# A two-block transformer kernel on one core: first gemm by passes, splits, context rows and stores in another order

## The chip, the cores and the metric

The kernel runs on one core of a Trainium2 chip. The time is that of the whole program on the device, in microseconds (us), as the median of several runs; less is better. A core has TensorE (PE in the profile; its weight loads are PEld), VectorE (DVE), ScalarE (ACT), GpSimd (POOL) and SyncE (SP), each with its own instructions in program order, tied together by semaphores. DMA queues bring data from memory to the on-chip SBUF. PE writes its products into eight PSUM banks.

## The reference

The inputs are float32. The first block takes x (256 rows of 1024) and computes, with an input norm, one projection `w_in` to six parts, chunkwise retention of 8 heads on q, k, v, a gated linear recurrence (RG-LRU) behind a causal convolution, and a product with `w_out` plus residual and a norm:

```python
xn = rms_norm(h, norm_in_g)
proj = einsum('btd,de->bte', xn, w_in)
...
h = h + einsum('bte,ed->btd', concatenate([y_ret, y_lru]), w_out)
return rms_norm(h, norm_out_g)
```

The second block has two layers over these 256 latent rows and 256 context rows. Each layer makes six modulation vectors (shift, scale and gain, twice) from the conditions, `silu(c) @ w_mod[l] + b_mod[l]`; then

```python
h = modulate(rms_norm_2(x, g_pre_mix[l]), sh1, sc1)
...(mLSTM, grouped attention and neighbourhood attention on h @ w_in[l])
o = merge_branches(y_ml, y_ga, y_na, zg, w_branch[l], w_out[l])
x = x + ga1 * rms_norm_2(o, g_post_mix[l])
f = conv_ffn(modulate(rms_norm_2(x, g_pre_ffn[l]), sh2, sc2), ...)
x = x + ga2 * rms_norm_2(f, g_post_ffn[l])
```

and the same for the context rows in layer 0. Layer 1 needs the latent rows alone behind its keys and values. The product of `ga` and the post-norm's weight is the "post-norm gain": a vector of 1024 for each of the latent and context rows (in layer 1, of the latent rows only).

## The kernel before

**Precision and pieces.** Every large product is done as three: both operands are split into a high part (fp32r) and the rest, and PE adds hi*hi, hi*rest and rest*hi. The weights come as a stream of 356 pieces of 512 KB (128 x 1024 float32, two blocks of 128 input rows by 512 columns) into a ring of four slots. SP issues a piece when the piece four before has been split to its low part (L728). ACT makes w_hi (`split_hi`, L1323; it waits for the piece to have landed and for PE to have used the piece four before), DVE makes w_lo (`split_lo`, L1959; it waits for w_hi). `split_hi(n)` makes all pieces below n that are not made yet, `ahead(key)` does so up to what PE needs soon. PE's `gemm` (matmul at L787) goes piece by piece, and for each pair of blocks does the three products one behind the other, so it needs w_hi, w_lo and both input parts before a piece. `gemm_by_groups` (L939), which serves the first w_in_2 chunks of a layer, goes in passes over a piece instead (all hi*hi, then the others), with norm transposes `norm_T` (L890, L892) between the groups.

**Order.** The order of every engine is written out by hand; nothing is planned at run time. The stages are: norm and w_in of the first block (to about 158 us), with retention and RG-LRU interleaved; w_out of the first block (to about 210 us); layer 0; layer 1 (from about 1100 us). Modulation vectors are made on DVE (L2015) from weight rows `mod_w` and `c_rows`, wherever DVE has room.

**Start.** PE warms up with WARM transposes of zeros (L824) and transposes the normed rows xn1 (L831), made on DVE in four halves (L1979). ACT evicts them to xT_hi (L1345) and DVE makes xT_lo (L1987), with a piece's split between any two. Then ACT does the recurrence's constants (L1347 to L1351), the split up to RING + 1 = 5 pieces, and silu of the conditions c_rows (L1354), for which DVE's first modulation products wait.

**First block's end.** Retention head h goes through DVE's statistics, ACT's root (`ret_sqrt`, L1410), DVE's norm and gate, PE's transposes (L871), ACT's `ret_mix` (L1416, mix_hi) and DVE's `ret_lo` (L2122, mix_lo). Pieces 48 to 63 are w_out. The context rows come by a DMA that ACT issues (L1490) after ret_sqrt(7); their squares and roots (L1497, L1499) stand on ACT after ret_mix(7), and `norm_right` on DVE (L2324, L2331; the right half row, and the reciprocal for the left half that ACT's `norm_left` L1505 makes) after the last retention head.

**Banks.** `take` (L597) hands out PSUM banks in rotation, six of them (0 to 5) for gemms, and waits until the bank has been drained. In the merge, `zg` chunks and branch products `br` take two banks each in turn; DVE drains the latter in `branch` (L2955, L2957).

**Post-norm gains.** DVE computes `gcol` (`post_gains`, L2312), 128 x 8 values per row kind. SP stores them transposed to memory (L701), as 1024 single elements of four bytes, behind the piece that `store_at` names, and reads them back as whole rows for all partitions (L714) behind the piece that `load_at` names, when they are wanted.

## Time and profile before

| | before |
|---|---|
| median of 3 runs | 1673.6 us |
| lowest and highest | 1673.26 and 1674.83 us |
| profiled execution, its own time | 1677.26 us |
| its span in the trace | 1675.6 us |
| busy PE / DVE / ACT | 1660.5 / 1240.1 / 847.2 us |

The profile is one execution. Its span runs from the first to the last instruction; the own time has 1.66 us around it. Busy time counts an engine's instructions; matmuls overlap, so a row with 0.28 us for a matmul of 256 columns can have the next one 0.12 us later. A row of the timeline has the start and the length in us, the engine, the line, the operation, what it writes and reads, its size and how many are run together; in brackets the idle time before it and what ended it. "Clock" is the granted clock of PE as a share of 2.4 GHz.

### The profile page before, as it was taken

To read this page: it belongs to the slowest core of one execution; us is meant where nothing else is said; L and a number is where in the kernel's file an instruction comes from. 1 tells how busy PE (TensorE), PEld (TensorE's weight loads), DVE (VectorE), ACT (ScalarE), POOL (GpSimd) and SP (SyncE) were. 2 spreads that over 40 slices of the span, in tenths; PEclk is the share of its full clock that TensorE was granted. 3 is DMA by queue.
4 is the path that set the end of the run, shared out by engine and by line. 5 is a ranking of instruction groups with operands and counts; after the bars stand their busy time and mean duration, and the time that the engine had idled before them with its cause. 6 is when DMAs were issued, how large, how long until landed. Compare 5 with 4: busy or idle time off the path is not lost.

```text
span 1675.6 us, 25213 instructions
## 1 busy us (share of the span) xinstructions
PE 1660.5 (99%) x9808; PEld 1426.9 (85%) x9808; DVE 1240.1 (74%) x2160; ACT 847.2 (51%) x1382; POOL 0.2 (0%) x4
## 2 busy tenths in 40 slices
PE   9999999999999999999999999999999999999998
PEld 9898888778887778889888888889788999989997
DVE  7999967966778897857878775347756776677874
ACT  6666555554334443256444442347553465575653
POOL 0000000000000000000000000000000000000000
PEclk9999999999999999999999999999999999999999
DMA  8657643132235346524555555324323554547563
GB/s 335 242 202 262 240 140 113 64 126 76 67 106 187 114 146 204 207 80 138 132 186 186 188 186 202 101 68 159 89 82 64 139 158 153 187 151 168 185 202 125
DMA packets 80230, 258.03 MB, mean 154 GB/s; under 512 B 14448, under 2 KB 18800, under 8 KB 79472
## 3 DMA queue, kind: packets, MB, share of 16 engines
q1 hardware_dynamic: 74352, 248.02, 45.8%
q10 hardware_dynamic: 5760, 8.39, 1.5%
q8 instruction: 79, 1.29, 0.3%
q14 instruction: 39, 0.32, 0.1%
HBM read 255.31 MB, written 1.07 MB: 153 GB/s over the span
## 4 chain that ended last, share of the span: by engine, by line
PE 89%; DVE 5%; ACT 3%; issue 1%; DMA 1%; ACTq 0%; DVEq 0%
PE bank L787 74%; PE bank L939 3%; PE bank L1117 2%; PE bank L1133 2%; PE bank L1105 2%; PE bank L1213 2%; DVE w_lo L1959 2%; ACT w_hi L1323 1%; DMA w_raw<-in_weights 1%; PE bank L1199 1%; DVE mod_w L2015 1%; DVE xc L2058 1%; PE bank L824 0%; PE bank L892 0%; PE bank L890 0%
## 5 line engine op out<-in xcount | busy, mean ns | idle before, releaser
L1959 DVE TENSOR_TENSOR w_lo<-w_raw,w_hi 128x1024 fp32r<-128x1024 f32 (+1 forms) x356 | 427.8, 1211 | 247.9 <-ACT w_hi L1323 246.5
L1323 ACT ACTIVATE w_hi<-w_raw 128x1024 fp32r<-128x1024 f32 (+1 forms) x356 | 370.1, 1048 | 335.7 <-PE bank L787 277.4
L787 PE MATMUL bank<-hT_hi,w_hi 128*128 128x512 f32 (+1 forms) x1280 | 447.5, 350 | 2.8 <-ACT w_hi L1323 2.3
L787 PE MATMUL bank<-hT_hi,w_lo 128*128 128x512 f32 (+1 forms) x1280 | 438.2, 342 | 0.0
L787 PE MATMUL bank<-hT_lo,w_hi 128*128 128x512 f32 (+1 forms) x1280 | 437.9, 342 | 0.0
L787 PEld LDWEIGHTS bank<-hT_hi,w_hi 128*128 128x128 f32 x1280 | 243.3, 190 | 31.1 <-ACT w_hi L1323 2.4
L787 PEld LDWEIGHTS bank<-hT_hi,w_lo 128*128 128x128 f32 x1280 | 243.2, 190 | 28.2
L787 PEld LDWEIGHTS bank<-hT_lo,w_hi 128*128 128x128 f32 x1280 | 243.5, 190 | 27.2 <-issue 1.0
L2015 DVE SCALAR_TENSOR_TENSOR mod_w<-mod_w,c_rows 128x1024 f32<-128x1024 f32 x102 | 124.3, 1219 | 8.5 <-DMA mod_w<-in_mod_weights 8.3
L787 PE MATMUL bank<-w_hi,hT_hi 128*128 128x512 f32 x272 | 114.3, 420 | 0.0
L787 PE MATMUL bank<-w_lo,hT_hi 128*128 128x512 f32 x272 | 106.7, 392 | 0.0
L787 PE MATMUL bank<-w_hi,hT_lo 128*128 128x512 f32 x272 | 106.5, 391 | 0.0
L2984 DVE SCALAR_TENSOR_TENSOR conv<-bank,vec,conv 128x510 f32<-128x510 f32 (+1 forms) x176 | 103.1, 612 | 3.5
L787 PE MATMUL bank<-w_hi,fT_lo 128*128 128x512 f32 x264 | 102.7, 389 | 0.0
L787 PE MATMUL bank<-w_hi,fT_hi 128*128 128x512 f32 x264 | 102.7, 389 | 0.0
L787 PE MATMUL bank<-w_lo,fT_hi 128*128 128x512 f32 x264 | 102.7, 389 | 0.0
L787 PE MATMUL bank<-xT_hi,w_hi 128*128 128x256 f32 x256 | 73.6, 287 | 1.8 <-DVE w_lo L1959 1.1
L787 PE MATMUL bank<-xT_hi,w_lo 128*128 128x256 f32 x256 | 72.4, 283 | 0.0
L787 PE MATMUL bank<-xT_lo,w_hi 128*128 128x256 f32 x256 | 72.4, 283 | 0.0
L1930 ACT ACTIVATE conv<-bank,vec 128x512 f32<-128x512 f32 (+1 forms) x88 | 56.1, 669 | 27.9 <-PE bank L787 26.6
L787 PE MATMUL bank<-yT_hi,w_hi 128*128 128x512 f32 (+1 forms) x192 | 66.6, 347 | 0.0
L2623 DVE TENSOR_REDUCE att<-bank 128x1 f32<-128x512 f32 (+1 forms) x96 | 54.6, 596 | 15.9 <-PE bank L1105 14.7
(399 smaller groups left out, 2707.7 us busy)
## 6 DMA issues: line engine op xcount, KB each, us to landing
w_raw<-in_weights SPq DMA_DIRECT2D x356, 512.0 KB, 4.2
mod_w<-in_mod_weights SPq DMA_DIRECT2D x102, 512.0 KB, 4.0
nbias<-in_window_bias ACTq DMA_DIRECT2D x32, 128.0 KB, 3.1
resid_c<-in_ctx ACTq DMA_DIRECT2D x2, 1024.0 KB, 5.5
gain_mix<-gain_rows SPq DMA_DIRECT2D x3, 512.0 KB, 5.7
gain_ffn<-gain_rows SPq DMA_DIRECT2D x3, 512.0 KB, 4.6
c_rows<-in_conditions SPq DMA_DIRECT2D x1, 1024.0 KB, 5.8
gatew<-in_gate_weights SPq DMA_DIRECT2D x1, 1024.0 KB, 11.4
```

The lines of the kernel that those rows point to most:

```text
L787: mm = pe.matmul(held[key][:, oc], st, mv_, start=(opens and k == 0 and t == 0 and i == 0), stop=(closes and k == tiles - 1 and t == 2), s ...
L939: mm = pe.matmul(held[key][:, o], st, mv_, start=opens, stop=(k == KD - 1 and t == 2), skip_group_check=True)
L1105: mm = pe.matmul(ps[j][:, score_at(g, t)], q_of(kind, q_lo, g + j, cols), k_of(kind, k_lo, g + j, n), start=(i == 0 and g == h), stop=(i = ...
L1117: mm = pe.transpose(ps[:, j * P:(j + 1) * P], prob[:, prob_of(h, t), j * P:(j + 1) * P], ident)
L1133: mm = pe.matmul(ps[i * HD:(i + 1) * HD, e // 2 * P:(e // 2 + 1) * P], v_[:, j, g * HD:(g + 1) * HD], turned_of(kind, l, e + i, t)[:, j * ...
L1213: mm = pe.matmul(ps[:, j * (P + 1):(j + 1) * (P + 1)], ml_w[:, d, s, t * P:(t + 1) * P], mv[:, s, h, :], start=(s == keys[0]), stop=(s == ...
L1323: a.activation(w_hi[:, p % RING, :, used], w_raw[:, p % RING, :].rearrange("p (k n) -> p k n", k=KP)[:, :, used], ACT.Copy).then_inc(hi_re ...
L1930: a.activation(conv[:, q, conv_cols(c)], psum(key)[:, j * nq:(j + 1) * nq], ACT.Identity, scale=V(f"ffn_w{l}", 2 * FB + blk), bias=V(f"ffn ...
L1959: v.tensor_tensor(w_lo[:, p % RING, :, used], w_raw[:, p % RING, :].rearrange("p (k n) -> p k n", k=KP)[:, :, used], w_hi[:, p % RING, :, ...
L2015: mm = v.scalar_tensor_tensor(product, w, 1.0, c_rows[:, s, :], ALU.mult, ALU.mult, accum_out=modT[:, l, j, s:s + 1])
L2623: v.tensor_reduce(att[:, h % 4, 0:1], ps[:, score_at(h, t)], AX.X, ALU.max, negate=True)\
L2984: v.scalar_tensor_tensor(dst, src, V(f"ffn_w{l}", tap * 2 * FB + blk), dst, ALU.mult, ALU.add)\
```

## The change

It has these parts, in the order of the diff.

- Start: WARM is 22 instead of 24. The left half of the second tile of xn1 is made on ACT, and the transposes wait for it. The first gemm, ("in", 0), is done by `gemm_first`: a piece in three passes (hi*hi, hi*rest, rest*hi), each with its own wait. On DVE, xT_lo stands ahead of w_lo for each pair.
- Pieces and conditions: ACT splits up to RING + 2 = 6 pieces ahead of silu of c_rows, and DVE splits the same ahead of the modulation products.
- Stores: in layer 1 the mix store goes behind piece ("w_in_2", 1, 4) instead of ("w_in_2", 1, 9), and the ffn store behind ("w_in_2", 1, 5) instead of ("w_up", 1, 4). The ffn gains use column 1 of gcol and are computed with the mix gains.
- Passes of `gemm_by_groups`: (0, "mix") takes hi*hi, hi*rest, rest*hi, where it took hi*hi, rest*hi, hi*rest. The others stay.
- Banks: the rotation is set to 4 ahead of merge(2).
- Context: the load is issued after ret_sqrt(6) instead of ret_sqrt(7); squares and roots stand ahead of split_hi(56), ret_mix(6) and ret_mix(7); the squares go to xn1 instead of sg. `norm_right` stands ahead of ret_lo(7).

```diff
@@ -120,7 +120,7 @@
 FIRST_MERGE = stream().index(("w_in_2", 0, 9, 0))
-WARM = 24
+WARM = 22
@@ -353,6 +353,11 @@
+    def gain_column(l, which):
...
+        return 1 if l and which == "ffn" else 0
...
@@ -698,13 +705,13 @@
                 for c in range(n):
-                    sp.dma_start(gain_rows[gain_index(l, which), c, :, :].rearrange("k p -> p k"), gcol[:, :, c], allow_slow_non_contiguous=True)\
+                    sp.dma_start(gain_rows[gain_index(l, which), c, :, :].rearrange("k p -> p k"), gcol[:, :, gain_column(l, which) + c], allow_slow_non_contiguous=True)\
...
-                sp.wait_ge(gain_stored, 16 * gain_loads(l, which))
+                sp.wait_ge(gain_stored, 16 * gain_loads(l, "ffn" if l else which))
@@ -715,9 +722,9 @@
             for l in range(LAYERS):
-                store_at[piece("w_in_2", l, 9)] = l, "mix"
+                store_at[piece("w_in_2", l, 4 if l else 9)] = l, "mix"
                 load_at[piece("w_out_2", 0, 0) + 4 if l == 0 else piece("w_in_2", l, 13) + 4] = l, "mix"
-                store_at[piece("w_up", l, 4)] = l, "ffn"
+                store_at[piece("w_in_2", l, 5) if l else piece("w_up", l, 4)] = l, "ffn"
@@ -825,6 +832,8 @@
                 pe.wait_ge(*xn_ready.at(("b1", g // 2)))
+                if g == 0:
+                    pe.wait_ge(*xn_left.at(0))
@@ -832,6 +841,34 @@
+            def gemm_first(banks):
...
+                at, n = pieces[0], KD // KP
+                for p in range(n):
+                    s = (at + p) % RING
+                    pieces[0] = at + p + 1
+                    pe.wait_ge(hi_ready, at + p + 1)
+                    pe.wait_ge(*xT_hi_ready.at(p))
+                    for t, (w, x) in enumerate(((w_hi, xT_hi), (w_hi, xT_lo), (w_lo, xT_hi))):
+                        if t == 1:
+                            pe.wait_ge(*xT_ready.at(p))
+                        if t == 2:
+                            pe.wait_ge(lo_ready, at + p + 1)
+                        for key, subs in banks:
+                            ps = psum(key) if p or t else take(pe, key)
+                            for i, (oc, wc, xcols) in enumerate(subs):
+                                for kk in range(KP):
+                                    k = p * KP + kk
+                                    mm = pe.matmul(ps[:, oc], w[:, s, kk, wc], x[:, k, xcols], start=(k == 0 and t == 0 and i == 0),
+                                                   stop=(k == KD - 1 and t == 2), skip_group_check=True)
+                            if t == 2 and key == banks[-1][0]:
+                                mm.then_inc(piece_used, 1)
+                                plan[("filled", key)] = ("piece", 0, at + n, at + n)
+                            elif t == 2 and p == n - 1:
+                                mm.then_inc(*filled(key))
+                                b, count = plan[("filled", key)][1:3]
+                                plan[("filled", key)] = ("bank", b, count, at + n)
@@ -903,7 +940,7 @@
                 whole, rest_x, rest_w = (w_hi, hT_hi), (w_hi, hT_lo), (w_lo, hT_hi)
-                passes = (whole, rest_x, rest_w) if l and which == "ffn" else (whole, rest_w, rest_x)
+                passes = (whole, rest_w, rest_x) if (l, which) in ((0, "ffn"), (1, "mix")) else (whole, rest_x, rest_w)
@@ -1020,7 +1057,7 @@
             late = Beside(retention_late(), RET_EVERY // 2, 2 * RET_SKIP)
-            gemm_T(("in", 0), xs, xT_hi, xT_lo, inputs=xT_ready.at)
+            gemm_first(blocks_T(("in", 0), 4, None, xs))
@@ -1265,6 +1302,7 @@
                 na.finish()
+                turn["rot"] = 4
@@ -1335,6 +1373,8 @@
             a.activation(rs[:, 0:2], ss[:, 0:2], ACT.Sqrt, scale=1.0 / D, bias=eps[:]).then_inc(*A.tell(root_ready, "b1"))
+            act.wait_ge(*xn_inv.at(0))
+            a.activation(xn1[:, 1, 0:COLS], resid[1][:, 1, 0:COLS], ACT.Copy, scale=rs[:, 3:4]).then_inc(*A.tell(xn_left, 0))
@@ -1349,7 +1389,7 @@
             a.activation(lam[:, 2, :], lam[:, 1, :], ACT.Ln, bias=1.0).then_inc(*A.tell(lam_ready, 0))
-            split_hi(RING + 1)
+            split_hi(RING + 2)
@@ -1482,22 +1522,22 @@
             ret_sqrt(6, False)
+            act.wait_ge(*drained_at(("rs", HEADS - 1)))
+            act.dma_start(resid[0][:], ctx_in).then_inc(ctx_loaded, 16)
...
             ret_sqrt(7, False)
-            act.wait_ge(*drained_at(("rs", HEADS - 1)))
-            act.dma_start(resid[0][:], ctx_in).then_inc(ctx_loaded, 16)
+            act.wait_ge(ctx_loaded, 16)
+            for t in range(NT):
+                a.activation(xn1[:, t, :], resid[0][:, t, :], ACT.Square, accum_out=ss[:, 56 + t:57 + t]).then_inc(*A.next())
+                act.wait_ge(*A.last())
+                a.activation(rs[:, 56 + t:57 + t], ss[:, 56 + t:57 + t], ACT.Sqrt, scale=1.0 / D, bias=eps[:])\
+                    .then_inc(*A.tell(root_ready, (0, "mix", t)))
...
             ret_mix(7)
-            split_hi(LAST_OUT)
-            act.wait_ge(ctx_loaded, 16)
-            for t in range(NT):
-                a.activation(sg[:, t, :], resid[0][:, t, :], ACT.Square, accum_out=ss[:, 56 + t:57 + t]).then_inc(*A.next())
-                act.wait_ge(*A.last())
-                a.activation(rs[:, 56 + t:57 + t], ss[:, 56 + t:57 + t], ACT.Sqrt, scale=1.0 / D, bias=eps[:])\
-                    .then_inc(*A.tell(root_ready, (0, "mix", t)))
@@ -1528,6 +1568,7 @@
                 norm_left(0, "mix", t)
+            split_hi(LAST_OUT)
@@ -1971,15 +2012,13 @@
             dve.wait_ge(*root_ready.at("b1"))
-            v.reciprocal(rs[:, 2:4], rs[:, 0:2]).then_inc(*W.next())
+            v.reciprocal(rs[:, 2:4], rs[:, 0:2]).then_inc(*W.tell(xn_inv, 0))
             dve.wait_ge(*W.last())
-            for half in range(2):
+            for half, t in ((0, 0), (1, 0), (1, 1)):
                 cols = slice(half * COLS, (half + 1) * COLS)
-                for t in range(NT):
-                    v.tensor_scalar(xn1[:, t, cols], resid[1][:, t, cols], rs[:, 2 + t:3 + t], None, ALU.mult)\
-                        .then_inc(*(W.tell(xn_ready, ("b1", half)) if t == NT - 1 else W.next()))
+                v.tensor_scalar(xn1[:, t, cols], resid[1][:, t, cols], rs[:, 2 + t:3 + t], None, ALU.mult)\
+                    .then_inc(*(W.tell(xn_ready, ("b1", half)) if t == half else W.next()))
             for g in range(KD // 2):
-                split_lo(g + 1)
@@ -1988,6 +2027,7 @@
                 W.mark(xT_ready, g)
+                split_lo(g + 1)
@@ -2156,6 +2196,7 @@
             split_lo(RING + 1)
+            split_lo(RING + 2)
@@ -2294,9 +2335,7 @@
             mod_ops(1)
-            ret_lo(7)
-            mod_ops(1)
-            mod_bias(0, 0, 16, 2, EARLY_MODS)
@@ -2314,8 +2353,8 @@
                 g_post = V(f"g_post_{which}{l}", 0, KD)
-                n = 2 if l == 0 else 1
-                v.tensor_tensor(gcol[:, :, 0:n], modT[:, l, 8 * (o + 2):8 * (o + 3), 0:n],
+                n, c0 = 2 if l == 0 else 1, gain_column(l, which)
+                v.tensor_tensor(gcol[:, :, c0:c0 + n], modT[:, l, 8 * (o + 2):8 * (o + 3), 0:n],
@@ -2368,11 +2407,15 @@
+            for t in range(NT):
+                norm_right(0, "mix", t)
+            ret_lo(7)
+            mod_ops(1)
+            mod_bias(0, 0, 16, 2, EARLY_MODS)
...
             norm_gains(0, "mix")
-            for t in range(NT):
-                norm_right(0, "mix", t)
             split_lo(LAST_OUT)
+            dve.wait_ge(*W.last())
@@ -2449,7 +2492,10 @@
                     norm_gains(*nxt)
-                    post_gains(*nxt)
+                    if nxt != (1, "ffn"):
+                        post_gains(*nxt)
+                    if nxt == (1, "mix"):
+                        post_gains(1, "ffn")
```

## Rows read from the trace of the kernel before

**Rows 1.** Page, part 1: engine, busy us (share), instructions.

```profile
PE 1660.5 (99%) x9808; PEld 1426.9 (85%) x9808; DVE 1240.1 (74%) x2160; ACT 847.2 (51%) x1382; POOL 0.2 (0%) x4
```

**Rows 2.** Waits of PE: line, what ended it, us, times, longest.

```profile
PE bank L787 <- ACT w_hi L1323: 2.3, 1, 2.3
...
PE bank L787 <- DVE w_lo L1959: 1.1, 3, 0.6
...
PE bank L939 <- DVE w_lo L1959: 0.9, 2, 0.5
```

**Rows 3.** Timeline, PE near 1525: start, length, instruction, idle before it.

```profile
1524.96 0.28 PE L787 MATMUL bank<-hT_hi,w_lo 128*128 128x256 f32 x1
1527.49 0.35 PE L787 MATMUL bank<-hT_hi,w_hi 128*128 128x256 f32 x1 [2.25 <-ACT w_hi L1323]
```

**Rows 4.** The same, ACT.

```profile
1523.95 1.06 ACT L1323 ACTIVATE w_hi<-w_raw 128x1024 fp32r<-128x1024 f32 x1 [7.71 <-DMA w_raw<-in_weights]
```

**Rows 5.** The same, SyncE's queue near 1510.

```profile
1510.15 0.43 SPq L701 DMA_DIRECT2D gain_rows<-gcol  x1
```

**Rows 6.** Stretches: each engine's busy us, granted clock, DMA share, GB/s.

```profile
1290.00:1304.00 14.00, 14.00 (x78) 12.12 (x77) 7.69 (x20) 3.06 (x4) 0.00 (x0) 1.00 0.83 65
...
1510.60:1523.90 13.30, 13.30 (x114) 13.30 (x113) 6.65 (x12) 4.56 (x7) 0.00 (x0) 1.00 1.02 102
...
1528.65:1532.06 3.41, 3.41 (x19) 3.41 (x18) 3.37 (x8) 3.29 (x7) 0.00 (x0) 0.50 0.77 245
```

**Rows 7.** Page, part 6: DMA issues, median us to landing.

```profile
w_raw<-in_weights SPq DMA_DIRECT2D x356, 512.0 KB, 4.2
```

**Rows 8.** Timeline, ACT in attention of layer 1.

```profile
1169.82 1.06 ACT L1323 ACTIVATE w_hi<-w_raw 128x1024 fp32r<-128x1024 f32 x1 [3.98 <-PE bank L787]
...
1188.59 1.06 ACT L1323 ACTIVATE w_hi<-w_raw 128x1024 fp32r<-128x1024 f32 x1
```

**Rows 9.** The same, DVE.

```profile
1188.74 0.69 DVE L2663 TENSOR_TENSOR gkT_lo<-bank,gkT_hi 128x512 fp32r<-128x512 f32 x1 [2.52 <-ACT gkT_hi L1792]
```

**Rows 10.** The same, PE.

```profile
1189.53 0.51 PE L1105 MATMUL bank<-gkT_hi,gqT_hi 64*128 64x512 f32 x2
```

**Rows 11.** Timeline, PE at layer 1's third merge.

```profile
1416.22 0.36 PE L787 MATMUL bank<-hT_hi,w_hi 128*128 128x256 f32 x1 [0.52 <-DVE ptmp L2955]
```

**Rows 12.** Timeline, PE in the first gemms.

```profile
11.68 0.35 PE L787 MATMUL bank<-xT_hi,w_hi 128*128 128x256 f32 x1 [0.78 <-DVE xT_lo L1987]
...
59.20 0.36 PE L787 MATMUL bank<-xT_hi,w_hi 128*128 128x256 f32 x1 [0.59 <-DVE w_lo L1959]
```

**Rows 13.** The same, DVE.

```profile
22.84 1.23 DVE L2015 SCALAR_TENSOR_TENSOR probT<-mod_w,c_rows 128x1024 f32<-128x1024 f32 x1 [2.00 <-ACT c_rows L1354]
```

**Rows 14.** Timeline, ACT, root of retention head 6.

```profile
175.83 0.20 ACT L1410 ACTIVATE bnst<-bnst 128x2 f32<-128x2 f32 x1 [2.85 <-DVE bnst L2094]
```

**Rows 15.** DMA issues between 180 and 190 us.

```profile
resid_c<-in_ctx ACTq DMA_DIRECT2D x1, 1024.0 KB, 6.3
```

**Rows 16.** Stretch with the context's squares and roots on ACT, as in 6.

```profile
193.45:196.31 2.86, 2.86 (x15) 2.33 (x13) 2.56 (x9) 2.77 (x7) 0.00 (x0) 1.00 0.96 339
```

**Rows 17.** Timeline, DVE, 185 to 197 us.

```profile
185.69 1.22 DVE L1959 TENSOR_TENSOR w_lo<-w_raw,w_hi 128x1024 fp32r<-128x1024 f32 x1
...
190.78 2.36 DVE L1959 TENSOR_TENSOR w_lo<-w_raw,w_hi 128x1024 fp32r<-128x1024 f32 x2
...
195.48 0.15 DVE L2324 RECIPROCAL ss<-rs 128x1 f32<-128x1 f32 x1
...
196.91 2.36 DVE L1959 TENSOR_TENSOR w_lo<-w_raw,w_hi 128x1024 fp32r<-128x1024 f32 x2
```

**Rows 18.** Timeline, PE, out product and first w_in_2 groups.

```profile
192.11 0.47 PE L787 MATMUL bank<-w_hi,mix_hi 128*128 128x512 f32 x1 [0.30 <-issue]
...
220.31 0.76 PE L939 MATMUL bank<-w_lo,hT_hi 128*128 128x272 f32 x4 [0.55 <-DVE w_lo L1959]
...
221.83 0.84 PE L890 MATMUL bank<-tab,sg 128*128 128x128 f32 x6 [0.26 <-ACT sg L1505]
```

More of the change, by code:

```diff
@@ L572, in build @@
     xn_ready = Counter("xn_ready")
+    xn_inv = Counter("xn_inv")
+    xn_left = Counter("xn_left")
     diag_ready = Counter("diag_ready")
@@ L588, in build @@
                qk_root, qk_ss, resid_ready, ret_hi, ret_root, ret_var, ret_y, root_ready, rows_ready, xT_hi_ready,
-               xT_ready, xn_ready, diag_ready, inv_ready, left_ready, right_ready, yT_hi_ready, yT_ready, gcol_ready, stat_ready, zo_ready, eps_ready)
+               xT_ready, xn_ready, xn_inv, xn_left, diag_ready, inv_ready, left_ready, right_ready, yT_hi_ready, yT_ready, gcol_ready, stat_ready, zo_ready, eps_ready)
     by_name = {c.name: c.sem for c in signals}
```

## The prediction

> **What bounds the kernel now.** I read the page first. TensorE (PE) is busy for 1660.5 us of a span of 1675.6, VectorE (DVE) for 1240 and ScalarE (ACT) for 847 [rows 1]. No edit takes a matmul away, save two of warm-up. So a change can only win time in which PE stands still or runs slowly, and that is 15 us at most, half of it before the first weight arrives. The second view is what PE waited for [rows 2]: one wait of 2.3 us for w_hi, three of 1.1 in sum and two of 0.9 in sum for w_lo, and little else. The third is PE's own order of time at each of these places, the fourth the engines that fed it there, and the last the stretches with DMA share and clock.
>
> The largest loss is late. A matmul starts at 1524.96 and the next at 1527.49, where 0.12 is the normal distance: 2.4 us lost [rows 3]. ACT had stood idle for 7.71 us until 1523.95, waiting for a weight piece from memory [rows 4]. SyncE had issued a post-norm store, gain_rows<-gcol, at 1510.15, right behind that piece [rows 5]. While it is under way the DMA engines are busy with a share of 1.02 and yet move only 102 GB/s [rows 6]: the store writes 1024 single elements of four bytes. The piece issued just ahead of it needed about 14 us (1509.8 to 1523.95), where a piece needs 4.2 in the median [rows 7]. Behind this gap PE runs for 3.41 us at a granted clock of 0.50, the lower level of 1.2 GHz [rows 6], half of which is lost: 1.7.
>
> **Part 1, the post-norm stores.** Layer 1's ffn store goes from the fifth w_up piece (1510) to a w_in_2 piece near 1177, its mix store from near 1290 to near 1161, one w_in_2 piece apart. At the old place nothing else is near: the 2.4 and the 1.7 go, **-4.1 us**. Next there is late nothing; pieces would land in their 4.2 us with ACT free. The old mix store cost no time: from 1290 to 1304 the share is 0.83 at 65 GB/s, and PE is busy for all 14.00 us [rows 6]. In the new place both stores come where a piece serves PE for a long time, since attention is interleaved: ACT's splits stand at 1169.82 (idle 3.98 us before, for PE) and 1188.59 [rows 8]. With the 14 us of a hit piece, the one issued at some 1161 lands near 1176 instead of 1166, the next one or two near 1178 and 1191. ACT works in program order, so the query copies gqT_hi behind the first of these splits and the key copies behind the third would be later, and there is no reserve: DVE makes the last low part of the keys from 1188.74 to 1189.43 [rows 9], and PE's first scores start at 1189.53 [rows 10]. Below: 0. Above: a stall and a clock loss as at 1527 for each store, 2 x 4.1. I take 0, by the store at 1290, because PE needs the piece issued at 1161 only at about 1188. The small extra product for column 1 of gcol is a DVE instruction of some 0.15 us (as the reciprocal in [rows 17]) beside slack.
>
> The Trainium skill, "DMA: Bandwidth & Descriptors", section "Why small descriptors are slow (HBM only)", speaks against this part: it names a fixed overhead of about three bus cycles for each packet and 32 bytes of metadata for each descriptor. By an estimate from that page, 1024 such elements over 16 engines are well under a microsecond of work, the 14 us would not be the store's, and the sum would be +0.8 instead of -3.3. The share of 1.02 at 102 GB/s and at 0.83 with 65 GB/s behind both stores [rows 6] says otherwise.
>
> **Part 2, bank order.** With turn["rot"]=4 before merge(2), layer 1's first zg chunk of the third merge no longer takes the two banks that the branch product has just filled. PE waited 0.52 us for the DVE drain there, and the first matmul after it took 0.08 longer [rows 11]: **-0.6**. In layer 0 the order turns as well, but the banks it now meets were drained 1 to 2 us before; 0, and at most the same 0.6 the other way.
>
> **Part 3, the start.** By passes, the first gemm needs only xT_hi and w_hi, so the 0.78 us of waiting for xT_lo [rows 12] goes, and the left half row of the second tile, made on ACT, takes an operation of about 0.5 off DVE (a norm_right is one with a reciprocal of 0.15 before it, and two take 1.28, [rows 17]) ahead of the transposes: 1.2 us earlier. But from 22.84 on DVE works without a break up to about 64 us, and the three waits for w_lo at L787 of [rows 2] lie in that stretch, the last and longest at 59.20 [rows 12]: the end of DVE's chain sets PE, not its start. What the chain starts with is silu of the conditions, for which DVE is idle 2.00 us [rows 13]. The sixth piece's split on ACT, 1.06 (as in [rows 4]), now stands ahead of it: chain +1.1. Its w_lo on DVE, 1.2, moves into that idle time: chain -1.2. Together 0. Swapping xT_lo ahead of w_lo also ends the first w_lo 0.9 to 1.6 later, and with them pieces five to eight are issued later, all inside the same hidden stretch if they land before 20. Bounds: -1.2 (advance kept) and +0.6 (the sixth piece lands late and holds silu). I take **0**: a 1.2 won at 11 and given back by 38 and 59 us.
>
> **Part 4, context load, squares, rows.** The load of the context is issued behind the sixth ret_sqrt, which ends at 176.03 [rows 14], and takes 6.3 us [rows 15]: landed 182.3. ACT now waits for it before w_hi of piece 55 and does squares and roots first, 2.86 us [rows 16]: to 185.1, then the split to 186.2. Queued behind the waiting instruction are that split, ret_mix(6) and the pieces after. DVE began w_lo of that piece at 185.69 [rows 17]: +0.5. Then the two norm_right, 195.48 to 196.91 less 0.15 idle = 1.28 [rows 17], stand ahead of ret_lo(7), and so ahead of the pair of w_lo at 190.78, the first of which PE awaited when it began piece 56 at 192.11 (0.30 idle) [rows 18]. PE starts there 0.5 + 1.3 = 1.7 later, near 193.8. About 0.3 comes back, as the rows that PE takes 6 us later are now ready early. What follows to the second tile of layer 0 (out product, residual, rows, transposes, 221.83 [rows 18]) is a chain from PE itself and moves along. **+1.4 us**. Bounds: -1.1 (waits of 0.30, 0.55 and 0.26 in [rows 18] vanish, nothing is added) and +2.
>
> **Part 5, pass order of the first w_in_2 groups.** (0, mix) now takes the third product (w_lo) last, so the 0.55 at 220.31 [rows 18] goes; but the next thing PE needs is the rows at 221.83, which are as late as before: 0 by itself, bounds -0.5 and +0.3 (hT_lo late in its place). Removed waits and the emptied warm-up cost nothing.
>
> **Sum**, for the profiled execution of 1677.26 us (span 1675.6 and 1.66 around it): -4.1 - 0.6 + 0 + 1.4 + 0 = -3.3, so 1673.9 to 1674.0. That execution stands 3.66 us above the median of the runs, 1673.6. If the difference is the profiler's, the median becomes 1670.3.
>
> **Rivals.**
> - *The late stall is not in ordinary runs.* 3.66 above the median is close to 4.1. For it: a landing time is what varies most. Against: the store's 1024 elements are issued in every run. Without any of it, -0.6 + 1.4 = +0.8: 1674.4; with the gap but no clock loss, -1.6: 1672.0. Chance 0.22.
> - *The middle and start win too.* The waits of [rows 18] vanish (-1.1) and the start keeps its 1.2: -4.1 - 0.6 - 1.1 - 1.2 = -7.0: 1666.6. For it: the waits stand there, and an earlier row or split is what ends each. Against: DVE has no gap to give it. Chance 0.20.
> - *Slower: the moved stores block ACT in layer 1's attention.* The piece ahead of each store takes 14 us, ACT stands in program order before gqT_hi and gkT_hi, and PE, with 0.1 of reserve at 1189.53, stalls and falls to 1.2 GHz. One such stall as at 1527 gives the 4.1 back: +0.8, 1674.4, no change. Two give +4.9, 1678.5. It decides from a piece at 1161 that lands after 1172. For it: two stores within 16 us. Against: [rows 6], the store at 1290 with PE busy throughout. Chance 0.13 for slower than the bound below.
> - *The start does not do what it says*, 1.2 up to 38 us and nothing after: that is in the forecast.
>
> **How the numbers follow.** 0.2% is 3.35 us, about what runs of this kernel can tell from no change: 1670.25 to 1676.95. Forecast 0.45 at 1670.3, which stands on the border, so half of it (0.22) is faster and half the same. Faster: 0.22 + 0.20 = 0.43. Same: 0.22 + 0.20 of the first rival = 0.43. Slower: the third and a rest of the first, 0.14. The range goes from the second rival's 1666.6 to 1674.6, just over the first rival's end, and leaves out 0.14 above and some 0.05 below. The forecast's own range is 1668.8 to 1672.2.
>
> **What would show it.** In the changed kernel's trace: no wait for w_hi over 1 us after 1500 and a granted clock of 1.00 there (part 1); no wait for ptmp in layer 1's merge (part 2); first weight matmul at 10.5 but the wait for w_lo near 38 and 59 longer (part 3); piece 56 begun at 193.8 with over 1.5 us of waiting for w_lo (part 4); no w_lo wait in (0, mix), one for the rows (part 5). The prediction is wrong if that piece begins before 192.5, if the time up to 100 us is over 0.8 shorter, or if PE waits over 1 us between 1165 and 1225.

## The result, and the profile after

Over 22 runs of each, the changed kernel takes 1678.26 us in the median (1674.94 to 1680.44) and the kernel before 1674.05 (1672.45 to 1677.55): ratio 1.0023, 95% interval 1.0017 to 1.0029. It is slower by 4.2 us, where 3.3 us faster was forecast. Yet the profiled executions stand the other way: 1676.76 us (span 1675.0) after, 1677.26 (span 1675.6) before. So the two traces can't be compared by their ends; they are compared stretch by stretch.

The page of the changed kernel, parts 1 and 6:

```profile
span 1675.0 us, 25206 instructions
PE 1658.2 (99%) x9804; PEld 1425.3 (85%) x9804; DVE 1239.4 (74%) x2159; ACT 848.8 (51%) x1383; POOL 0.2 (0%) x4
...
c_rows<-in_conditions SPq DMA_DIRECT2D x1, 1024.0 KB, 7.1
```

Its waits of PE, to be read against [rows 2] (L794 was L787, L976 was L939, L927 was L890):

```profile
PE bank L794 <- issue: 3.7, 2, 3.1
PE bank L794 <- DVE w_lo L2000: 2.7, 4, 1.1
...
PE bank L927 <- ACT sg L1545: 0.7, 1, 0.7
PE bank L976 <- DVE w_lo L2000: 0.4, 1, 0.4
```

The wait of 2.3 us for w_hi is gone, and in its place stands one of 3.1 us, and 2.7 instead of 1.1 for w_lo. PE's timeline has the places:

```profile
10.48 0.36 PE L863 MATMUL bank<-xT_hi,w_hi 128*128 128x256 f32 x1
...
29.09 0.36 PE L794 MATMUL bank<-xT_hi,w_hi 128*128 128x256 f32 x1 [1.09 <-DVE w_lo L2000]
...
60.65 0.35 PE L794 MATMUL bank<-xT_hi,w_hi 128*128 128x256 f32 x1 [0.58 <-DVE w_lo L2000]
...
196.31 0.47 PE L794 MATMUL bank<-w_hi,mix_hi 128*128 128x512 f32 x1 [3.14 <-issue]
...
225.75 0.52 PE L927 MATMUL bank<-tab,sg 128*128 128x128 f32 x3 [0.75 <-ACT sg L1545]
...
1193.43 0.50 PE L1142 MATMUL bank<-gkT_hi,gqT_hi 64*128 64x512 f32 x2
```

The first matmul is 1.2 us earlier than in [rows 12]; at 60.65 PE is 1.45 late, at 196.31 (against 192.11 in [rows 18]) 4.2, at 225.75 (221.83) 3.9, and at 1193.43 (1189.53, [rows 10]) still 3.9. The loss is made in two places, 11 to 60 us and 176 to 196 us. In layer 1 the third merge has no wait for ptmp as in [rows 11], which is worth 0.8 (PE's lateness falls from 3.9 to 3.1), and near 1525 there is no stall and no slow clock as in [rows 3] and [rows 6] (-4.0): 3.9 - 0.8 - 4.0 = -0.9. ACT's last read of a bank starts at 1668.89 instead of 1669.74, 0.85 earlier, of which the spans keep 0.6.

**Start.** The issues of the conditions and of the sixth piece by SyncE, before and after:

```profile
11.15 0.43 SPq L734 DMA_DIRECT2D c_rows<-in_conditions  x1
12.71 0.33 SPq L728 DMA_DIRECT2D w_raw<-in_weights  x1
```

```profile
12.73 0.43 SPq L741 DMA_DIRECT2D c_rows<-in_conditions  x1
14.28 0.33 SPq L735 DMA_DIRECT2D w_raw<-in_weights  x1
```

The sixth piece landed at 18.3 (5.6 us after its issue) before and at 21.1 (6.8 us) after. ACT, then DVE, of the changed kernel:

```profile
21.11 1.06 ACT L1361 ACTIVATE w_hi<-w_raw 128x1024 fp32r<-128x1024 f32 x1 [1.70 <-DMA w_raw<-in_weights]
22.19 1.28 ACT L1394 ACT_TABLE_LOAD   x1
23.48 1.92 ACT L1394 ACTIVATE c_rows<-c_rows 128x2048 f32<-128x2048 f32 x1
```

```profile
22.20 1.22 DVE L2000 TENSOR_TENSOR w_lo<-w_raw,w_hi 128x1024 fp32r<-128x1024 f32 x1 [1.54 <-ACT w_hi L1361]
25.43 1.23 DVE L2055 SCALAR_TENSOR_TENSOR probT<-mod_w,c_rows 128x1024 f32<-128x1024 f32 x1 [2.00 <-ACT c_rows L1394]
```

ACT waits 1.70 us for the sixth piece, with silu behind it in program order. DVE's chain starts at 25.43 instead of 22.84 [rows 13]: 2.6 late, less the one w_lo now done before it, 1.14: 1.45, the delay at 60.65. It is more than executions differ by: this wait ends at 60.15 to 60.89 in the five traces with the whole new start (after, e1, e13 to e15) and at 58.48 to 59.62 in the eleven with the old one.

**Middle.** ACT and DVE:

```profile
184.88 1.06 ACT L1533 ACTIVATE xn<-resid_c 128x1024 f32<-128x1024 f32 x1 [1.43 <-DMA resid_c<-in_ctx]
...
187.63 1.04 ACT L1361 ACTIVATE w_hi<-w_raw 128x1024 fp32r<-128x1024 f32 x1
```

```profile
188.71 1.22 DVE L2000 TENSOR_TENSOR w_lo<-w_raw,w_hi 128x1024 fp32r<-128x1024 f32 x1 [1.59 <-ACT w_hi L1361]
...
195.00 2.35 DVE L2000 TENSOR_TENSOR w_lo<-w_raw,w_hi 128x1024 fp32r<-128x1024 f32 x2
```

The context landed at 184.86, 7.7 us after its issue at 177.19, not 6.3. All that the forecast queued behind it follows: w_hi of piece 55 at 187.63, DVE idle 1.59, the first w_lo of the pair done at 196.1, PE at 196.31. DVE's 1.59 and the 1.2 of the two half rows (193.81 to 195.00) make the 2.75 us that PE loses here on top of the start's 1.45.

### The profile page after: what moved, and what is told of

Its sections match the earlier page's. It is cut to its first block, busy times and chain, and to the rows that moved or that the text cites. A ratio compares the mean times of both kernels' runs of the same rounds, so it can differ in the third digit from the quotient of the medians.

```text
span 1675.0 us, 25206 instructions
## 1 busy us (share of the span) xinstructions
PE 1658.2 (99%) x9804; PEld 1425.3 (85%) x9804; DVE 1239.4 (74%) x2159; ACT 848.8 (51%) x1383; POOL 0.2 (0%) x4
## 4 chain that ended last, share of the span: by engine, by line
PE 90%; DVE 5%; ACT 2%; issue 1%; DMA 0%; ACTq 0%; DVEq 0%
PE bank L794 75%; PE bank L976 3%; PE bank L1154 2%; PE bank L1170 2%; PE bank L1142 2%; PE bank L1250 2%; DVE w_lo L2000 1%; PE bank L1236 1%; ACT w_hi L1361 1%; DVE mod_w L2055 1%; DVE xc L2098 1%; PE bank L831 0%; PE bank L929 0%; PE bank L927 0%; DMA w_raw<-in_weights 0%
## 5 line engine op out<-in xcount | busy, mean ns | idle before, releaser
L794 PE MATMUL bank<-hT_hi,w_hi 128*128 128x512 f32 (+1 forms) x1280 | 446.6, 349 | 0.0
L794 PE MATMUL bank<-hT_hi,w_lo 128*128 128x512 f32 (+1 forms) x1280 | 437.6, 342 | 0.0
L794 PE MATMUL bank<-hT_lo,w_hi 128*128 128x512 f32 (+1 forms) x1280 | 437.3, 342 | 0.0
L794 PEld LDWEIGHTS bank<-hT_hi,w_hi 128*128 128x128 f32 x1280 | 242.6, 190 | 28.1 <-issue 1.7
L794 PEld LDWEIGHTS bank<-hT_hi,w_lo 128*128 128x128 f32 x1280 | 242.5, 189 | 28.2
L794 PEld LDWEIGHTS bank<-hT_lo,w_hi 128*128 128x128 f32 x1280 | 242.8, 190 | 27.0 <-issue 1.0
L794 PE MATMUL bank<-w_hi,hT_hi 128*128 128x512 f32 x272 | 114.3, 420 | 0.0
L794 PE MATMUL bank<-w_lo,hT_hi 128*128 128x512 f32 x272 | 106.7, 392 | 0.0
L794 PE MATMUL bank<-w_hi,hT_lo 128*128 128x512 f32 x272 | 106.5, 391 | 0.0
L794 PE MATMUL bank<-w_hi,fT_hi 128*128 128x512 f32 x264 | 102.7, 389 | 0.0
L794 PE MATMUL bank<-w_hi,fT_lo 128*128 128x512 f32 x264 | 102.7, 389 | 0.0
L794 PE MATMUL bank<-w_lo,fT_hi 128*128 128x512 f32 x264 | 102.7, 389 | 0.0
L794 PE MATMUL bank<-xT_hi,w_hi 128*128 128x256 f32 x224 | 64.6, 288 | 3.3 <-DVE w_lo L2000 2.7
L794 PE MATMUL bank<-yT_hi,w_hi 128*128 128x512 f32 (+1 forms) x192 | 66.6, 347 | 0.0
L794 PE MATMUL bank<-yT_hi,w_lo 128*128 128x512 f32 (+1 forms) x192 | 64.7, 337 | 0.0
L794 PE MATMUL bank<-yT_lo,w_hi 128*128 128x512 f32 (+1 forms) x192 | 64.6, 336 | 0.0
```

Of the source, the lines that this page charges most:

```text
L794: mm = pe.matmul(held[key][:, oc], st, mv_, start=(opens and k == 0 and t == 0 and i == 0), stop=(closes and k == tiles - 1 and t == 2), s ...
```

## Experiments

Ratios are of medians to before, measured beside it on the same chip in five rounds, with the 95% interval in brackets. There were four such sessions, in which the kernel before had medians of 1674.45 (e1 to e4), 1673.96 (e5 to e8), 1674.13 (e9 to e12) and 1674.03 us (e13 to e16); a difference in us is to the one of its own session. Each experiment starts from the kernel before unless it says otherwise.

**e1_start: the start alone.** Edit, all hunks of the start, in short:

```diff
-WARM = 24
+WARM = 22
...
-            gemm_T(("in", 0), xs, xT_hi, xT_lo, inputs=xT_ready.at)
+            gemm_first(blocks_T(("in", 0), 4, None, xs))
...
-            split_hi(RING + 1)
+            split_hi(RING + 2)
...
-                split_lo(g + 1)
...
                 W.mark(xT_ready, g)
+                split_lo(g + 1)
```

> The start of the changed kernel alone (passes, left half row on ACT, low part of the inputs ahead of the low part of the weights, sixth piece ahead of the conditions); all else as before. Theory A (from the two traces: the sixth piece lands at 21.1 instead of 18.3 us, so silu of the conditions ends 2.5 us later and the vector engine's chain behind it 1.4 later): +1.4 us against before, and the third wait for w_lo ends near 60.6 instead of 59.2. Rival B (the start is neutral, as forecast; the loss in the trace of the changed kernel is an accident of that execution): 0 us, third wait ends near 59.2.

1678.7 us, ratio 1.0023 (1.0013 to 1.0034): +4.2 us, three times what theory A expected. PE's timeline:

```profile
60.81 0.36 PE L789 MATMUL bank<-xT_hi,w_hi 128*128 128x256 f32 x1 [0.58 <-DVE w_lo L1993]
...
201.61 0.41 PE L922 MATMUL bank<-tab,sg 128*128 128x128 f32 x2 [2.17 <-ACT sg L1539]
```

The 60.81 is theory A's. The 2.17 is new: in the old order the context's squares stand on ACT behind splits of weight pieces, and those pieces landed late beside the context, which took 8.6 us itself (ACT waited 6.04, 1.23 and 0.19 us for pieces between 186 and 196 us). That wait of PE is in the kernel before too, about 0.2 us in its first trace (PE goes on at 197.89) and 1.93 in its second (e12, where ACT waited 3.61 us for a piece).

**e2_sixth: only the two splits.**

```diff
-            split_hi(RING + 1)
+            split_hi(RING + 2)
...
             split_lo(RING + 1)
+            split_lo(RING + 2)
```

> Only the sixth piece's two splits ahead of silu and of the modulation products; the order of the low parts as before, so the sixth piece lands near 18.3 us and ACT does not wait for it. Theory A (what costs is the late landing): silu ends 1.05 later, a w_lo of 1.14 is out of the chain, sum -0.1, wait near 59.1. Rival B (the place of the split costs by itself): +1 us or more.

1673.46 us, 0.9992 (0.9984 to 1.0001). The wait ends at 58.71. The piece landed at 19.1, before ACT had finished the fifth. The place of the split costs nothing when the piece is there.

**e5_nosixth and e6_noswap: the start without the sixth piece; the start with w_lo ahead of xT_lo as before.** e5 keeps split_hi(RING + 1); e6, against the start of e1:

```diff
             for g in range(KD // 2):
+                split_lo(g + 1)
                 dve.wait_ge(*xT_hi_ready.at(g))
```

> The start of the changed kernel (passes, left half row on ACT, low part of the inputs ahead of the low part of the weights) without the sixth piece ahead of silu. Theory A (the cost of e1_start is that silu stands in order behind a split that waits for a late piece): silu ends near 22.6 as before, the third w_lo wait ends at 59.2 +- 0.3, time 0 to +0.5 us against before. Rival B (the later issue of pieces five to eight costs by itself): the wait ends at 60 or later, +1 us or more.

> The start of the changed kernel with the sixth piece, but with each low part of the weights ahead of the low part of the inputs, as before. Theory A (the swap delays the low parts and so the issue of the sixth piece): pieces issued and landed as before (18.3), silu ends near 23.9, the wait ends near 58.9, -0.3 us against before. Rival B (sixth piece and passes themselves cost): the wait ends at 60.5, +1.4.

Waits end at 59.18 and 58.88, as theory A has them, where e1 has 60.81:

```profile
59.18 0.36 PE L789 MATMUL bank<-xT_hi,w_hi 128*128 128x256 f32 x1 [0.58 <-DVE w_lo L1993]
```

```profile
58.88 0.36 PE L789 MATMUL bank<-xT_hi,w_hi 128*128 128x256 f32 x1 [0.60 <-DVE w_lo L1993]
```

So the loss of the start needs both edits: the swap, which makes the sixth piece late (it landed at 21.1 in the changed kernel, and at 19.3 in e6, in time for ACT), and the split placed ahead of silu, which makes silu wait for it. The ordinary runs are at 1675.77, 1.0012 (1.0003 to 1.002), and 1674.92, 1.0006 (0.9997 to 1.0015): +1.8 where 0 to +0.5 was expected, and +1.0 where -0.3 was. That rest stays open, as no trace shows it in the start.

**e3_middle: context load, squares and rows forward.** Edit: the diff's hunks 1482, 1528, 2294 and 2368, of which

```diff
             ret_sqrt(7, False)
+            act.wait_ge(ctx_loaded, 16)
...
             split_hi(56)
...
+            for t in range(NT):
+                norm_right(0, "mix", t)
+            ret_lo(7)
```

> Only the context load, the squares and the rows moved forward. Theory A (the load shares the DMA engines with two weight pieces and lands 7.7 us after its issue, ACT stands in order before w_hi of piece 55): +2.5 us, PE begins piece 56 near 194.9 instead of 192.1. Rival B (forecast: landing in 6.3 us): +1.4, piece 56 near 193.8. Rival C: 0 or less.

1678.26 us, 1.0021 (1.0012 to 1.003), +3.8 us; the load landed after 8.2 us:

```profile
195.85 0.47 PE L787 MATMUL bank<-w_hi,mix_hi 128*128 128x512 f32 x1 [3.27 <-issue]
```

Theory A named the cause and was too low by 1 us in the place and by 1.3 in the time. Part of that is a slow clock that this trace does not have (see e14).

**e8_squares: the same, but the split and ret_mix(6) ahead of the wait.** Against e3:

```diff
-            act.wait_ge(ctx_loaded, 16)
-            for t in range(NT):
...
             split_hi(56)
             ret_mix(6)
+            act.wait_ge(ctx_loaded, 16)
+            for t in range(NT):
...
```

> As e3_middle, but w_hi of piece 55 and the sixth head's output stand ahead of the wait for the context and of its squares. Theory A (e3_middle's loss is 2.2 us of ACT's order plus 1.3 us of the two right half rows ahead of the low parts): 2.2 us of it go, piece 56 begins 1.2 to 1.5 later than before (193.4), +0.8 us against before. Rival B (the half rows alone make it): piece 56 at 195.5 or later, +3.5. Rival C (they cost nothing): 0 or less.

1674.39 us, 1.0004 (0.9995 to 1.0012). With the same 8.2 us to land, the stall is 1.47:

```profile
194.84 0.47 PE L787 MATMUL bank<-w_hi,mix_hi 128*128 128x512 f32 x1 [1.47 <-issue]
```

1.47 less 0.30 as before is the 1.2 of the two half rows; 3.27 less 1.47 is the 1.8 of ACT's order. (The start time is 1.4 us later than the 193.4 expected: PE had lost 1.5 us between 138 and 170 us, before the edit acts.)

**e7_load: only the issue moved.**

```diff
             ret_sqrt(6, False)
+            act.wait_ge(*drained_at(("rs", HEADS - 1)))
+            act.dma_start(resid[0][:], ctx_in).then_inc(ctx_loaded, 16)
             ret_mix(4)
...
             ret_sqrt(7, False)
-            act.wait_ge(*drained_at(("rs", HEADS - 1)))
-            act.dma_start(resid[0][:], ctx_in).then_inc(ctx_loaded, 16)
```

> Only the issue of the context load moved ahead (behind the root of head 6), squares and rows as before. Theory A (what costs in e3_middle is that ACT waits for the load ahead of w_hi of piece 55, not the load itself; and landing some 5 us earlier takes the load off pieces 58 and 59, for which ACT waits before the squares): piece 56 begins at 192.1, the rows' wait near 198 goes, -0.5 us. Rival B (the earlier load holds weight pieces that PE wants): piece 56 later than 193, +1 us.

1673.55 us, 0.9998 (0.9989 to 1.0006). It landed after 8.2 us as well, and PE lost nothing by it:

```profile
192.48 0.47 PE L787 MATMUL bank<-w_hi,mix_hi 128*128 128x512 f32 x1 [0.28 <-issue]
```

The small wait for the rows near 198 is not in this trace.

**e4_late and e10_bank: layer 1's stores and the bank order; the bank order alone.** e4 has the diff's store and post_gains hunks and this line, e10 the line alone:

```diff
                 na.finish()
+                turn["rot"] = 4
                 merge(2)
```

> Only layer 1's stores moved and the rotation set to 4 ahead of the third merge. Theory A (the stall of 2.4 us and the slow clock behind it near 1525 are not in ordinary runs of before): -0.7 us. Rival B (they are in each run, and the new place costs nothing): -4.7 us. Rival C (the new place costs as much): above 0.

> Only the rotation set to 4 ahead of the third merge. Theory A (the drained banks are worth the 0.68 us of the wait near 1416, and the rest of e4_late's -1.4 is the stores' rare stall): -0.7 us, no wait at the third merge of layer 1, store stall possible at 1525. Rival B (the stores are worth nothing in ordinary runs): -1.4 us, as e4_late.

1673.07 us, 0.9991 (0.9982 to 1.0), and 1673.46, 0.9993 (0.9985 to 1.0002): -1.4 and -0.7 us. The 4.1 us of the forecast are not there. Eleven traces have the stores in the old place (before, e1 to e3, e5 to e8, e10 to e12); PE stalls near 1525 in the first only. In e10 the same store delays the pieces and ACT waits, and PE doesn't:

```profile
1516.96 1.06 ACT L1324 ACTIVATE w_hi<-w_raw 128x1024 fp32r<-128x1024 f32 x1 [0.53 <-DMA w_raw<-in_weights]
1523.04 1.06 ACT L1324 ACTIVATE w_hi<-w_raw 128x1024 fp32r<-128x1024 f32 x1 [4.50 <-DMA w_raw<-in_weights]
```

The piece ahead of the store landed after 7.0 us here, after 14.2 in the first trace [rows 4, 5], and after 4.2 to 10.9 in the nine others; up to 10.9 there is reserve. Whether the stores' move is worth the 0.7 us by which e4 and e10 differ can't be told from these intervals.

**e11_passes: the pass order of (0, mix) alone.**

```diff
-                passes = (whole, rest_x, rest_w) if l and which == "ffn" else (whole, rest_w, rest_x)
+                passes = (whole, rest_w, rest_x) if (l, which) in ((0, "ffn"), (1, "mix")) else (whole, rest_x, rest_w)
```

> Only the order of the passes of the first w_in_2 groups of layer 0. Theory A (PE's wait of 0.55 for w_lo near 220 goes, and the rows it needs next are as late as before, so the wait moves there): 0 +- 0.3 us, rows' wait near 222 longer by 0.5. Rival B (the wait is saved): -0.5 us.

1675.1 us, 1.0009 (1.0 to 1.0018). In the place it is theory A, a wait for w_lo of 0.1 and then

```profile
223.72 0.52 PE L890 MATMUL bank<-tab,sg 128*128 128x128 f32 x3 [0.74 <-ACT sg L1505]
```

where [rows 18] have 0.55 and 0.26. That ordinary runs are 1 us slower isn't explained by it. The trace, at 1675.5 us, is 1.05 us late on ACT already at 170.72 (169.67 before), and PE waits 0.93 for the context's first rows near 200. Both lie ahead of the edit's place, so neither can be put down to it.

**e12_before: the kernel before again.**

> The kernel before once more, for a second trace. Theory A (the stall near 1525 is rare): no wait for w_hi there, a span near 1671.6 to 1672.8, and the context load's landing differs from the first trace's 6.3 us. Rival B: the stall is there again, span near 1675.6.

A single execution of 1677.3 us, span 1675.6 as the first one, but for another reason. Nothing near 1525; instead the context landed after 7.4 us, ACT waited 3.61 for a piece beside it, and

```profile
199.99 0.30 PE L890 MATMUL bank<-tab,sg 128*128 128x128 f32 x1 [1.93 <-ACT sg L1505]
```

```profile
200.62:204.03 3.41, 3.41 (x15) 3.22 (x14) 3.41 (x6) 1.79 (x3) 0.00 (x0) 0.50 0.76 233
```

(the second a stretch, with the granted clock third from the end): 1.9 us of waiting, and 3.41 us at 1.2 GHz behind it.

**e13_after and e14_after: the changed kernel again, twice.**

> The changed kernel once more, for a second trace. Theory A (the third of a us by which its ordinary runs lie above the sum of the two losses in its trace is a slow clock behind the stall near 193, present in a part of the executions, and a later landing of the context): stall of 3 to 4 us before piece 56, and in this or the next trace a granted clock of 0.50 for some 3.4 us behind it. Rival B: no such stretch in either, and another stall that the first trace does not have.

> The changed kernel a third time; expectations as for e13_after.

1679.94 and 1677.75 us. Landings of 8.7 and 6.9 us, stalls of 3.27 and 2.37, and in both the slow clock that the first trace does not have:

```profile
198.54:201.95 3.41, 3.41 (x9) 2.65 (x9) 3.30 (x9) 0.02 (x1) 0.00 (x0) 0.50 0.71 281
```

```profile
195.27:198.68 3.41, 3.41 (x8) 2.71 (x9) 3.30 (x9) 1.06 (x2) 0.00 (x0) 0.50 0.64 201
```

```profile
196.31:199.70 3.39, 3.39 (x15) 2.79 (x16) 3.28 (x9) 1.12 (x2) 0.00 (x0) 1.00 0.60 191
```

(the last is the first trace's, at full clock, 15 matmuls in 3.4 us and not 8 or 9). e14's stall is below the 3 to 4 us expected, as its load landed sooner.

How often the slow clock comes can be read from the ordinary executions, as each has a mean granted clock. In the traces this mean is 0.9978 to 0.9985 with such a stretch and 0.9989 to 0.9997 without, so a mean that the results round to 0.998 or less points to one (some that round to 0.999 may have one too). It was 0.998 or less in 13 of the 22 executions of the changed kernel, in 8 of 11 of e3 and 7 of 11 of e16, in none of e8, e9 and e15 (11 each), and in 3 of the 111 of the kernel before in the four sessions. So it goes with the changed middle. Of these 111 only 5 took 1676.8 us or more, where the two traced executions of before, each with a stall and a slow clock, took 1677.3: both are unusual ones.

**e15_midback, e16_startback, e9_best: a two by two.** e15 is the changed kernel with e7's middle; e16 the changed kernel with the old start and the sixth piece; e9 the sixth piece, the late part and e7's load.

> The changed kernel with its middle put right: only the issue of the context load ahead, squares and rows as before. Theory A (start costs 1.45, middle 2.5 and a part of the slow clock, bank order gives 0.7): third w_lo wait ends near 60.6, no stall over 0.5 us before piece 56 and at the rows, time 1.4 - 0.7 - 0.4 = +0.3 us against before. Rival B (the two losses are one loss, seen twice): +2 us or more.

> The changed kernel with its start put back to that of before (but for the sixth piece); middle as changed. Theory A: third wait ends near 59, stall of 3.3 us before piece 56, time +3.8 (as e3_middle) - 1.0 - 0.7 = +2.1 us against before. Rival B (the middle's loss needs the late start): 0 or less.

> The parts that measured faster, together: sixth piece ahead of silu, stores and bank order of layer 1, and only the issue of the context load moved ahead. Theory A (their effects are in different stretches and add up: -1.0, -1.4 and -0.4): -2.5 us against before. Rival B (the first two contain the same rare stall or noise): -1 us or less.

| | middle as e7 | middle as changed |
|---|---|---|
| start as before, sixth piece | e9: 1672.71, 0.999 (0.9981 to 0.9999) | e16: 1677.27, 1.0019 (1.001 to 1.0028) |
| start as changed | e15: 1674.53, 1.0002 (0.9993 to 1.001) | 1678.26, 1.0023 (1.0017 to 1.0029) |

Each against its own before, the changed middle costs 3.7 and 4.7 us, the changed start 1.9 and 1.0. The middle's loss is there with either start. The start's is of the size of the intervals in this table; that it is there with either middle is shown by the traces: the wait ends at 60.89 in e15 and at 58.48 in e16. (e9 has the old pass order, which is all else by which the cells differ.) e16's trace has a stall of 3.23 us and the slow clock behind it; it measured +3.2 us where +2.1 was expected, e15 +0.5 where +0.3 was. e9 beats both kernels, by 1.4 us before and 5.6 after, but the -2.5 expected of it is missed: the three gains that single runs had shown do not add up.

## Why the prediction was wrong

- **The steps that failed.** The stores' term of -4.1 is near nothing in ordinary runs, which leaves +0.8 of the forecast. The start's 0 is +1.45, and the middle's +1.4 is +2.5 with +1.0 for a slow clock that the sum does not have. The change is slower by these two.
- **Bound and method.** Right: only PE's waits and its clock moved, and each wait was found where the rows had put its cause.
- **Part 1, stores (-4.1).** This step failed first: the term counts a stall and a slow clock that ordinary runs seldom have. They were in one of eleven traces of kernels with the old place, and e4, which moves the stores, gained 0.7 us over e10, which doesn't, and that is not clear of noise. The forecast had this as a rival with 0.22, and had the clue in hand: the profiled execution stood 3.66 above the median. The new place cost PE nothing in the changed kernel's traces (1193.43 stands 3.9 late as 225.75 does; no wait between 1165 and 1225 in any of the three), though a piece issued ahead of the second store took 12 us in the first; the slower rival's mechanism is not in them.
- **On the rule.** The small-descriptor figures of the Trainium skill ("DMA: Bandwidth & Descriptors", section "Why small descriptors are slow (HBM only)") would, by the prediction's estimate, make the store too short to delay a piece. The traces disagree: at the old place the piece ahead of the store needed 4.2 to 14.2 us, and the one behind it 9.5 to 15.4 in the ten traces that have its landing, where the median of all pieces is 4.2.
- **Part 2, banks (-0.6).** Right: 0.8 in the traces of after and e10, and 1673.46 against 1674.13 in e10's ordinary runs, though that is within its interval.
- **Part 3, start (0, bounds -1.2 and +0.6).** Wrong by 1.45, outside its bound, though the bound names the mechanism. The first half held (first matmul at 10.48, advance given back by DVE's chain). What failed is the assumption that pieces issued later are hidden "if they land before 20": the sixth landed at 21.1. The swap moved the issue of the fifth piece from 10.78 to 12.36, when the first four had landed (12.0) and the DMA engines stood idle, and with it that of the sixth from 12.71 to 14.28: 1.6 of its 2.8 us. For the rest, the 1 MB of conditions in front of the sixth took 7.1 us instead of 5.8. That is not the swap's: it took 6.9 to 7.4 in all seven traces with the new first gemm, e6 without the swap among them, and 5.6 to 5.9 in the eleven others; why stays open. e5 and e6 show that silu's place behind this piece turns the lateness into a loss.
- **Part 4, middle (+1.4, bounds -1.1 and +2).** Mechanism right, size wrong. Its term for ACT's order, 0.5, was 1.6 in the changed kernel's first trace and 1.8 between e3 and e8, as the load took 6.9 to 8.7 us in the new place and not 6.3: DVE stood idle for w_hi of piece 55 for 0.82, 1.59 and 2.17 us in e14, after and e3, where it took 6.9, 7.7 and 8.2. The term for the half rows, 1.3, was 1.2. (The two terms add to 1.8; the prediction wrote 1.7.) And a term was missing: a stall of 2 to 3 us can bring 3.41 us at the lower clock, 1.7 us, here in two of the changed kernel's three traces and in at least 13 of its 22 ordinary executions.
- **Part 5, passes (0).** Right in the place.
- **Signs.** None of the three signs of being wrong came: piece 56 began at 196.31, the time up to 100 us was longer, and PE did not wait over 1 us between 1165 and 1225. All three look for less or for part 1's rival; none looks for a start or a middle that is later than forecast.
- **Sum.** With what was measured: +1.45 (start), +2.5 (middle, net of the rows' wait), -0.8 (banks), and 13 of 22 times 1.7 for the clock, +1.0: +4.15, against 4.2 measured. That it comes out so near is in part luck: e1 alone measured +4.2 and e3 alone +3.8, so the parts do not simply add in ordinary runs.

Open: 1 to 3 us in the ordinary runs of e1, e5 and e6 beyond what their edits do in the start. Later landings around the context load in the old order, up to 2.17 us of waiting and in e12 the slow clock with it, are a candidate: in e1 the trace has the wait, for e5 (0.60 us of it in the trace) and e6 (0.39) it is argued and not shown. Open too is why executions differ by up to 1.5 us between 138 and 170 us (e8, e11).

## What to carry to other kernels

Before a wait of a trace is priced, hold the profiled execution's own time against the median: what it stands above (3.66 us here, for a wait priced at 4.1) may well not be in ordinary runs. Never put a wait for a transfer, on an in-order engine, ahead of work whose reserve is smaller than the spread of that transfer's landing; issue it early and wait late, as e7 does. And an edit that delays the release of a buffer delays every load issued behind it, so ask which engine will stand in order behind the last of them, as silu did here.

## What the runs showed of the hardware

The 1 MB load of the context took 6.2 to 8.6 us to land in nine traces with its issue in the old place, and 6.9 to 8.7 in nine with the new one. A PE stall of 1.9 to 3.3 us was followed by 3.41 us at a granted clock of 0.50 in the first trace of before, e12, e13, e14 and e16, and by no slow clock in the changed kernel's first trace, e1 and e3: the same stall can cost 1.7 us more or not. Beside a store of 1024 four-byte elements, at one place of the program, the 512 KB piece ahead of it landed after 4.2 to 14.2 us and the one behind it after 9.5 to 15.4; PE waited once in eleven traces.
